# Gate units between the pair matrices and the inverses, an earlier decay chain, four gate buffers, and inverse roots by logarithm and exponent, in a two-layer hybrid trunk

## What is computed

```python
# one input projection of rms_norm(x), split among four branches and four sigmoid gates
# A: gated DeltaNet, chunks of 64
q, k = l2_normalize(q), l2_normalize(k)
g = -exp(a_log) * softplus(a + dt_bias)
gc = cumsum(g)                                  # within a chunk
m = where(strict, (k*beta) @ k.T * decay, 0)
t_inv = (eye + m)^-1                            # triangular
u, w = t_inv @ (v*beta), t_inv @ (k*beta*exp(gc))
# scan over chunks, then rms_norm(o) * silu(z)
# B: latent attention: rms_norm of the q and kv latents
# C: RWKV-7: l2_normalize(k * k_k), a delta rule with vector decay, group norm of o per head
# D: top-k sparse attention
out = w_o @ sum_b(sigmoid(gate_b) * (w_out_b @ branch_b))
x = x + out;  x = x + mlp(x)
```

## Time and profile before

| | us |
|---|---|
| median of 3 runs | 2272.09 (2271.6 to 2272.57) |
| the profiled execution | 2271.29 |
| its span in the profile | 2269.5 |
| PE busy | 2128.6 (94%) |
| DVE busy | 1238.7 (55%) |
| POOL busy | 732.9 (32%) |
| ACT busy | 720.8 (32%) |

### The profile page before, as it was taken

How to read it: one execution, slowest core, us unless ns; L and a number is a source line. 1 busy time by engine, 2 the same in 40 slices (tenths; PEclk the granted TensorE clock), 3 DMA queues, 4 the chain that set the end, 5 groups by cost and what they waited for, 6 DMA issues and landing times.

```text
span 2269.5 us, 34623 instructions
## 1 busy us (share of the span) xinstructions
PE 2128.6 (94%) x14488; PEld 1647.5 (73%) x14488; DVE 1238.7 (55%) x1930; ACT 720.8 (32%) x1100; POOL 732.9 (32%) x550
## 2 busy tenths in 40 slices
PE   5989899998999999999989898899899999999997
PEld 3778577765666788888868776877565678888886
DVE  6885765897563422222358766569956544222223
ACT  3421321332333332323243133123243334323322
POOL 1530221332213444444434012123223044444442
PEclk7999899998999999999989999999999999999998
DMA  4320111221121233332332001112212123323321
GB/s 159 106 70 15 56 30 41 82 68 58 45 96 61 84 111 97 97 93 94 94 105 90 27 26 55 36 60 71 64 54 97 34 81 99 95 93 95 100 93 65
DMA packets 52266, 170.03 MB, mean 75 GB/s; under 512 B 5648, under 2 KB 13968, under 8 KB 51600
## 3 DMA queue, kind: packets, MB, share of 16 engines
q1 hardware_dynamic: 50928, 162.75, 22.4%
q0 software_dynamic: 1184, 5.07, 0.6%
HBM read 160.45 MB, written 7.34 MB: 74 GB/s over the span
## 4 chain that ended last, share of the span: by engine, by line
PE 74%; DVE 21%; ACT 2%; issue 2%; DMA 1%; SPq 0%; DVEq 0%; ACTq 0%
PE bank_a L464 10%; PE bank_a L465 10%; PE bank_a L468 10%; PE bank_v L468 7%; PE bank_v L464 7%; PE bank_v L465 6%; PE bank_v L604 5%; PE bank_v L526 3%; DVE arena L1350 3%; DVE arena L1777 3%; DVE m L1775 2%; PE bank_v L720 2%; PE bank_v L702 1%; DVE arena L1768 1%; DVE mg L1356 1%
## 5 line engine op out<-in xcount | busy, mean ns | idle before, releaser
L425 POOL TENSOR_TENSOR w_lo<-ring,w_hi 128x512 fp32r<-128x512 f32 x536 | 726.4, 1377 | 1366.3 <-ACT w_hi L1064 1366.2
L464 PE MATMUL bank_a<-h_hi,w_hi 128*128 128x512 f32 x1376 | 561.3, 408 | 17.7 <-ACT w_hi L1064 12.5
L465 PE MATMUL bank_a<-h_lo,w_hi 128*128 128x512 f32 x1376 | 542.4, 394 | 0.0
L1064 ACT ACTIVATE w_hi<-ring 128x1024 fp32r<-128x1024 f32 x268 | 281.6, 1051 | 235.0 <-DVE arena L1892 220.5
L468 PE MATMUL bank_a<-h_hi,w_lo 128*128 128x512 f32 x1376 | 341.2, 390 | 0.0
L464 PEld LDWEIGHTS bank_a<-h_hi,w_hi 128*128 128x128 f32 x1376 | 261.5, 190 | 96.9 <-issue 18.0
L465 PEld LDWEIGHTS bank_a<-h_lo,w_hi 128*128 128x128 f32 x1376 | 262.3, 191 | 60.6 <-issue 8.1
L468 PEld LDWEIGHTS bank_a<-h_hi,w_lo 128*128 128x128 f32 x1376 | 259.1, 188 | 54.8 <-POOL w_lo L425 0.7
L1350 DVE TENSOR_TENSOR sg<-bank_v,sg 128x512 f32<-128x512 f32 x112 | 77.5, 692 | 339.6 <-PE bank_v L468 256.9
L464 PE MATMUL bank_v<-parts,w_hi 128*128 128x512 f32 x640 | 254.5, 398 | 1.4 <-DVE parts L1863 1.4
L465 PE MATMUL bank_v<-parts,w_hi 128*128 128x512 f32 x640 | 253.4, 396 | 0.0
(11 more groups left out here) (284 smaller groups left out, 2539.6 us busy)
## 6 DMA issues: line engine op xcount, KB each, us to landing
ring<-in_w SPq DMA_DIRECT2D x268, 512.0 KB, 3.5
out_ring<-in_w SPq DMA_DIRECT2D x64, 128.0 KB, 3.5
x_dram<-arena SPq DMA_DIRECT2D x2, 2048.0 KB, 7.6
arena<-x_dram SPq DMA_DIRECT2D x2, 2048.0 KB, 7.7
arena<-in_x SPq DMA_DIRECT2D x2, 1024.0 KB, 8.8
arena<-tabs POOLq DMA_DIRECT2D x4, 512.0 KB, 4.0
out_x<-arena SPq DMA_DIRECT2D x2, 1024.0 KB, 4.2
par<-in_par POOLq DMA_DIRECT2D x2, 937.0 KB, 7.2
```

Of the source, the lines that this page charges most:

```text
L425: ins = nc.gpsimd.tensor_tensor(w_lo[:, g % SPLIT, ks, :], raw, w_hi[:, g % SPLIT, ks, :].bitcast(F32), ALU.subtract)
L464: mm(b[:], w_hi[:, s, k, :], hi[:, k, :], start=k == 0, stop=False)
L465: mm(b[:], w_hi[:, s, k, :], lo[:, k, :], start=False, stop=False)
L1064: act_fn(w_hi[:, g % SPLIT, :, :], ring[:, g % RING, :, :], ACT.Copy).then_inc(S["split_hi"], 1)
```

## The change

- **Order of PE.** The first gate unit of the RWKV branch moves from behind the scan to between the second and the third pair call. The other gate units move up: after the scan come gates 1, 2 and 3 (three units where four were). Gate 7 of the RWKV branch moves behind the delta branch's pair calls, and the outputs of gates 6 and 7 follow it. `unit_list` is reordered to match, and ACT's and DVE's lists too.
- **Order of DVE.** `first_steps` is a function of its own. For the RWKV branch it runs after the second pair call's masks, ahead of the masks of `ark` and `arb`; for the delta branch after its masks, ahead of the merge of gates 6 and 7. The decay chain (L1675 to L1683) moves ahead of the first rule: its first part before the third convolution, its second behind the last; ACT's softplus moves behind the eviction of the fourth convolution input. The wide copies move ahead of the first merges.
- **Buffers.** `sg` has four tiles where it had two, and ACT waits for merge n - 4.
- **Head sums.** The five groups of sums (`r_l2`, `r_gv`, `g_l2`, `g_gv`, `m_nv`) go to a banks. ACT takes `Ln` with scale and epsilon straight from the bank and then one `Exp` with scale -0.5. DVE's scaling and reciprocal instructions and ACT's `Sqrt` are gone. In the delta branch's output norm this stands one unit earlier in ACT's list.
- The program is built with `dynamic_dma_scratch_size=8192`, and two constant columns are added. In layer 0 ACT waits once for the constants.

```diff
 def unit_list():
     u = [("rw", i) for i in range(8)] + [("misc", i) for i in range(2)]
-    u += [("gd", i) for i in range(8)]
-    u += [("merge", 2, i) for i in range(8)]
+    u += [("gd", i) for i in range(6)] + [("merge", 2, 0)]
+    u += [("gd", i) for i in range(6, 8)]
+    u += [("merge", 2, i) for i in range(1, 8)]
...
-        sg = sb("sg", [P, 2, T])
+        sg = sb("sg", [P, GATES, T])
...
                 pair_matrices(R["kd"], R["et"], "r")
+                numbers = [gate(l, 2, 0)]
                 pair_matrices(R["kd"], R["rt"], "r")
...
                 block_sums(l, "r_o", NC, R["o"], 2, "r_mean")
-                numbers = [gate(l, 2, 0)]
-                block_sums(l, "r_sq2", 1, R["sq"], 2, "r_gv")
                 numbers.append(gate(l, 2, 1))
-                block_sums(l, "g_sq", 1, G["sq"], 4, "g_l2")
-                more = gates(l, 2, 1)
+                block_sums(l, "r_sq2", 1, R["sq"], 2, "r_gv", "a")
+                more = [gate(l, 2, 2)]
+                block_sums(l, "g_sq", 1, G["sq"], 4, "g_l2", "a")
+                more.append(gate(l, 2, 3))
                 pe.wait_ge(S["r_out"], at(l, "r_out", 1))
...
                 merge(l, 2, 0, 2)
-                merge(l, 2, 0, 3)
+                numbers = [gate(l, 2, 6)]
                 pe.wait_ge(S["g_prep"], at(l, "g_prep", 1))
                 transposes((G["et"], G["vb"], G["bh"]), "g")
                 pair_matrices(G["co"][:, 2:4, :], G["kb"], "g")
                 pair_matrices(G["co"][:, 2:4, :], G["co"][:, 0:2, :], "g")
+                numbers.append(gate(l, 2, 7))
+                merge_outputs(0, numbers)
                 invert(l, "g", G, lambda n: None)
...
+            def inverse_roots(dst, scales, eps, sums, roots):
+                for i, scale in enumerate(scales):
+                    act.wait_ge(a_full, filled.next())
+                    b = filled.bank()
+                    act_fn(dst[:, i, :], b[:], ACT.Ln, scale=scale, bias=cst(eps)).then_inc(S[sums], 1)
+                act.wait_ge(S[sums], sums_done(sums, len(scales)))
+                act_fn(dst, dst, ACT.Exp, scale=-0.5).then_inc(S[roots], 1)
...
                     act_fn(G["ci"][:, i, :], b[:], ACT.Copy).then_inc(S["g_in"], 1)
                     split_next()
+                    if i == 3:
+                        act_fn(gsm[:, 5, :], ab[:, :, 4:8], ACT.Sigmoid)
+                        act.wait_ge(S["g_t1"], at(l, "g_t1", 1))
+                        act_fn(gsm[:, 1, :], gsm[:, 1, :], ACT.Exp).then_inc(act_step, 1)
+                        act_fn(sml[:, 8:12], pr("a_log"), ACT.Exp).then_inc(S["g_t2"], 1)
+                        act.wait_ge(act_step, l + 1)
+                        act_fn(gsm[:, 1, :], gsm[:, 1, :], ACT.Ln, bias=1.0).then_inc(S["g_sp"], 1)
...
-                merge_sig(l)
-                merge_sig(l)
+                merge_sig(l, 1)
+                inverse_roots(R["sq"], (1.0 / C, 1.0 / C), "gn_eps", "r_gv", "r_gs")
+                merge_sig(l, 1)
+                inverse_roots(G["rs"], (1.0,) * 4, "eps", "g_l2", "g_l2s")
+                merge_sig(l, 1)
...
                 for c in range(6):
+                    if c == 2:
+                        dve.wait_ge(S["ab_in"], at(l, "ab_in", 1))
+                        th = lambda i: gsm[:, i, :].rearrange("p (t h) -> p t h", h=H)
+                        tt(th(0), ab[:, :, 0:4], pr("dt").unsqueeze(1).to_broadcast([P, TT, H]), ADD)
+                        v.scalar_tensor_tensor(gsm[:, 1, :], gsm[:, 0, :], -1.0, gsm[:, 0, :], MUL, ALU.min).then_inc(S["g_t1"], 1)
+                        dve.wait_ge(S["g_t1"], reached("g_t1"))
+                        ts(ab[:, :, 8:16], ab[:, :, 8:16], float((8 * 64) ** -0.5), None, MUL)
                     conv(c)
+                dve.wait_ge(S["g_sp"], at(l, "g_sp", 1))
+                stt(gsm[:, 2, :], gsm[:, 0, :], 0.0, gsm[:, 1, :], ALU.max, ADD)
+                stt(th(4), th(2), -1.0, sml[:, 8:12].unsqueeze(1).to_broadcast([P, TT, H]), MUL, MUL)
                 masked("r", R["u"], lambda hp: wide("before_c"))
                 dve.wait_ge(S["r_tok"], at(l, "r_tok", 8))
                 masked("r", R["akk"], lambda hp: wide("before_c"))
+                first_steps("r", R)
                 masked("r", R["ark"], lambda hp: wide("upto_c"))
                 masked("r", R["arb"], lambda hp: wide("upto_c"))
...
-                    v.tensor_scalar(R["sq"][:, f, :], b[:], 1.0 / C, GN_EPS, MUL, ADD).then_inc(S["r_gv"], 1)
-                    dve.wait_ge(S["r_gv"], reached("r_gv"))
-                v.reciprocal(R["sq"], R["sq"]).then_inc(S["r_gr"], 1)
...
-                link(v.reciprocal(G["rs"][:, 2:4, :], G["rs"][:, 2:4, :]))
...
-    nc = bacc.Bacc("TRN2", target_bir_lowering=False, num_devices=1)
+    nc = bacc.Bacc("TRN2", target_bir_lowering=False, num_devices=1, dynamic_dma_scratch_size=8192)
```

More of the change, by code:

```diff
@@ L685, in scan, with block_sums @@
                     fill(c)
-            def block_sums(l, need, k, src, tiles, done):
+            def block_sums(l, need, k, src, tiles, done, pool="v"):
                 pe.wait_ge(S[need], at(l, need, k))
                 for i in range(tiles):
-                    b, reader, emptied = banks.next("v", done)
+                    b, reader, emptied = banks.next(pool, done)
                     pe.wait_ge(reader, emptied)
-                    mm(b[:], cst("blocks"), src[:, i, :], start=True, stop=True).then_inc(v_full, 1)
+                    mm(b[:], cst("blocks"), src[:, i, :], start=True, stop=True).then_inc(a_full if pool == "a" else v_full, 1)
             def attention(l, x, q_of, k_of, v, fill):
@@ L889, in _ @@
                 pe.wait_ge(S["m_sq"], at(l, "m_sq", 1))
-                b, reader, emptied = banks.next("v", "m_nv")
+                b, reader, emptied = banks.next("a", "m_nv")
                 pe.wait_ge(reader, emptied)
@@ L893, in _ @@
                     ins = mm(b[:], cst("ones"), Mv["sq"][:, k, :], start=k == 0, stop=k == 1)
-                ins.then_inc(v_full, 1)
-                b, reader, emptied = banks.next("v", "m_nv")
+                ins.then_inc(a_full, 1)
+                b, reader, emptied = banks.next("a", "m_nv")
                 pe.wait_ge(reader, emptied)
-                mm(b[:], cst("ones"), Mv["sq"][:, 2, :], start=True, stop=True).then_inc(v_full, 1)
+                mm(b[:], cst("ones"), Mv["sq"][:, 2, :], start=True, stop=True).then_inc(a_full, 1)
                 merge(l, 3, 0, 2)
@@ L1052, in late_sig @@
                     n = sigs[0]
[L1053 removed]
+                    act_fn(sg[:, n % GATES, :], sg[:, n % GATES, :], ACT.Sigmoid).then_inc(S["mg_sig"], 1)
                     sigs[0] += 1
@@ L1143, in _ @@
                 take_low_rank("g", None)
+                inverse_roots(R["tmp"], (1.0, 1.0), "eps", "r_l2", "r_l2s")
                 take_rw(5)
-                act.wait_ge(S["r_l2r"], at(l, "r_l2r", 1))
-                act_fn(R["tmp"], R["tmp"], ACT.Sqrt).then_inc(S["r_l2s"], 1)
                 take_rw(6)
@@ L1417, in invert @@
                     dve.wait_ge(S[x + "_x1"], reached(x + "_x1"))
+            def invert(l, x, V, fill):
+                halves = [slice(half * M // 2, (half + 1) * M // 2) for half in range(2)]
                 for n, s in enumerate(LEVELS):
@@ L1576, in _ @@
                 mix(4)
-                for f in range(2):
-                    dve.wait_ge(v_full, filled.next())
-                    b = filled.bank()
-                    v.tensor_scalar(R["tmp"][:, f, :], b[:], EPS, None, ADD).then_inc(S["r_l2"], 1)
-                    dve.wait_ge(S["r_l2"], reached("r_l2"))
-                v.reciprocal(R["tmp"], R["tmp"]).then_inc(S["r_l2r"], 1)
-                dve.wait_ge(S["r_l2r"], reached("r_l2r"))
                 mix(5)
@@ L1725, in _ @@
                 dve.wait_ge(S["g_sq2"], reached("g_sq2"))
-                for f in range(2):
-                    dve.wait_ge(v_full, filled.next())
-                    b = filled.bank()
-                    v.tensor_scalar(G["sq2"][:, f, :], b[:], 1.0 / C, EPS, MUL, ADD).then_inc(S["g_gv"], 1)
-                    dve.wait_ge(S["g_gv"], reached("g_gv"))
-                v.reciprocal(G["sq2"], G["sq2"]).then_inc(S["g_gr"], 1)
-                dve.wait_ge(S["g_gr"], reached("g_gr"))
                 dve.wait_ge(S["g_gs"], at(l, "g_gs", 1))
```

108 lines of the change are left out of this document (38 added, 70 removed).

## The result

The changed kernel takes 2219.24 us (median of 4 runs, 2217.08 to 2219.4) beside 2272.33 us for the kernel before in the same session: ratio 0.9762, 95% interval 0.9749 to 0.9774. The forecast was 2216, the range 2203 to 2236. 53 us are gone where 56 were forecast.

The account below looks back on a forecast made before the run. PE, busy 94% of the span, was taken as the bound. Per layer 1.9 (gap one) + 5.44 (unit) + 20.1 (gap two's stalls) + 0.4 = 27.8 us, twice 55.7, gave 2216 us, range 2203 to 2236.

Parts of the forecast that it names:

- Gap two: PE's stretch from RWKV scan to delta inverse: stalls gone, gain 20.1 us a layer, plus 5.44 for the moved unit.
- all three stalls: In gap two: w_hi 5.12 us plus 2.2 cold; decay tiles 6.19 plus 2.8; before the inverse 3.6 plus 1.8.
- The one new wait: At the fourth g_l2 sum, PE waits for a bank that ACT empties late: 1.6 us a layer.
- Gap one: PE ahead of the RWKV inverse: 14.0 us shrinks to 12.1 with a gate unit inside, gaining 1.9 a layer.
- The rest: Outside both gaps: only the L859 wait behind the delta output norm goes, 0.4 us a layer; other parts 0.
- L702 stays: At the attention's start: DVE bounds up to there, so PE's wait of 9.3 us in 4 stays unchanged.
- the 0 for the buffers: Four gate buffers free ACT from merges but gain PE nothing beyond the w_hi waits: 0 us.
- become late: Rival, chance 0.24: ACT's in-order queue runs late; 5 us a layer gives 2226, 10 us gives 2236.
- its two figures: By the skill's rules: drains at table switches make the sum 2227; one load for exp and ln lowers it 2.6 us.
- Only displaces: Rival, chance 0.07: DVE's masks come 5 us later, PE still waits, gap one gives nothing: 2231.
- the slower one: Rival, chance 0.03: smaller scratch brings the first parameter load in portions, delaying DVE's first norm; 16 portions give 2299.
- DVE's lead carries on: Rival, chance 0.15: DVE's 4.7 us lead from the delta output norm reaches the top-k: 2207.

Follow-up runs that it names:

- g1: Changed kernel with three gate buffers in place of four: 2218.11 us, ratio 0.9753 to the kernel before.
- u2: Changed kernel with the r_gv and g_l2 head sums again through DVE's addition and reciprocal and ScalarE's root: 2245.66 us, ratio 0.9877.
- u5: Changed kernel with the sums of the delta output norm and latent norms again through DVE's reciprocal and ScalarE's root: 2217.67 us, ratio 0.9761.
- s2: Changed kernel with the first index scores, their rectifications and the fourth rotation product one unit earlier: 2218.4 us, ratio 0.9756.
- u1: Changed kernel with the gate unit between the RWKV pair matrices put back behind the scan: 2226.53 us, ratio 0.979.
- c1: The kernel before with only the smaller scratch for POOL's DMA descriptors: 2273.31 us, ratio 1.0003.
- second profile: Profile of the changed kernel run again unedited in another session: 2217.73 us, ratio 0.9761 to the kernel before.
- s4: Changed kernel with later q/k sums, all index scores ahead of outputs, selections ahead of merges, latent units ahead of second outputs: 2233.1 us, ratio 0.9826.
- s1: Changed kernel with three q/k sums moved behind the fourth gate unit and the last between the two outputs: 2214.8 us, ratio 0.9741.

## Why the prediction was right

- **Gap two, its stalls and the unit (5.44 + 20.1 = 25.5 us a layer forecast).** Measured 24.9 and 25.7. Here the time was, and all three stalls went with their cold clock. The one new wait came at the place and with the size worked out (1.66 us; forecast 1.6), so the working of ScalarE's order held: the root was ready at 240.3 us, forecast 239.2, and the sums ahead of it start 1.08 us later too (240.83, in the old times 239.75). The output chain took 5.9 us (240.41 to 246.27), not 8.5; no wait hung on it.
- **Its parts.** Undone one at a time, unit, sums, decay chain and last gate cost 6.4, 26.1, 12.0 and 5.9 us, together 50 of the 54 us (0.0238 of 2272), each known to some 4 us: no large overlap shows. The buffers' share does not show in the total (g1). The prediction was right that the w_hi wait is ScalarE's root held by DVE's reciprocal. What failed is u2's expectation that it comes back at the same place: it moved to the outputs.
- **Gap one (1.9 us a layer).** From the second pair call to DVE's first level step it is 12.08 us (152.89 to 164.97; forecast 12.1), partly by luck: the decay chain cost DVE some 1 us less than taken, and an instruction beside POOL's split 1 us more. The inverse behind it adds small waits. From the transposes to the end of the inverse, the two layers gained 0.5 and 2.9 us in the first profile, 1.8 and 2.3 in the second (51.7 and 52.6 before).
- **The rest (0.4 a layer).** From delta to the last output matmul of the attention (L723) layer 0 gained 1.1 us and layer 1 lost 0.8: PE waits longer ahead of the scores (L705) and 1.6 us a layer less at L713 behind them. The wait L859 went as forecast (0.8 us in 2), but the index scores' waits grew by 0.6 in both layers together. By u5 none of it is the output norm's. The reason given (DVE bounds from the selection to the attention) was half right: s2 shows that PE takes a lead of DVE away once more, at the first output. "L702 stays" and the 0 for the buffers were wrong steps that cancel: g1 shows that the fourth buffer lengthens the wait ahead of the attention and shortens the attention by about as much. That they cancel is luck.
- **The rivals.** ScalarE did not become late: its new waits are 1.66 us at the sums and 0.77 at the delta transposes. The Trainium skill's drain of 1.38 us behind a table load (ScalarE: Activation LUTs, What ACT_TABLE_LOAD costs) is not in this trace: load at 240.33, sigmoid at 241.62. One load for exp and ln, as the same page has it (Table sets: the hidden batching unit), did not come either, so neither of its two figures (2227, 2.6 us less) came. "Only displaces" fell with u1, the slower one with c1, "DVE's lead carries on" with u5.
- **The 3 us short of the forecast.** In the profiled execution some 2.8 us are lost by the end of the RWKV inverse of layer 0, which another execution of the same kernel lacks; but that one's span is only 1.3 us shorter, so at most a part of the shortfall is this. The 1 to 1.8 us between delta and attention in both layers are the fourth buffer's: they are there with the old output sums (u5: 179.5 and 180.7 us), are all but gone with three (g1: 177.0 and 178.3), and the attention gives about as much back. The shortfall of the medians stays in part unexplained; it is about as large as the measurement's doubt.
- **The range and the signs.** The lower end of the range is 2203, but the sum beside it gives 2201; its 10.2 us of cold clock and the upper end's "low bounds" are not worked out, so the range rests on less than the forecast. Of the signs, L705 is not unchanged (11.7 us against 9.3), and a wait of 2.56 us for w_hi stayed, at 56.4 us, outside both gaps. The end of the delta inverse came 23.9 us earlier in layer 0, and 26.7 in the second profile; the sign said some 27.

## What to carry to other kernels

When a slow operation of one engine (here a reciprocal of 6.55 us) feeds several consumers, PE's waits name whichever stands first in PE's order; price the operation, not the wait. A lead gained on an engine off the critical path is worth what its next inputs allow: follow it to the next place where it needs the bound engine before counting it, and test it, since moving that place can cost more than it brings (s4). A wait made by an order of work over few banks could here be had back by placing other work between (s1, 2 us a layer). A run without an effect on the total can hide two effects: compare its stretches as well (g1).

## What was not expected of the hardware

An elementwise DVE instruction with both inputs in SBUF (128x512) took 1.67 us in place of 0.69 when it started beside POOL's split of w_lo, in the second profile 1.69; the four masks behind it, with one input in PSUM, took 2.87 us together (0.72 each), though the first of them still ran beside POOL. The Trainium skill (GPSIMD Engine Reference, 1. Specifications) says that GpSimd shares its way to SBUF with VectorE and contends with instructions of two SBUF inputs; the trace agrees. The same happens ahead of the attention (g1 above): a scan of 512 columns took 2.17 us in place of 1.23.

A DVE instruction of 16 columns took 0.18 us at its new place, with POOL idle, and 1.18 us in the kernel before, while POOL worked on w_lo (265.94 to 270.88 us). So a small instruction's duration in one profile was a bad price for others of its kind.

The same unit behind a short wait had the clock at 1.00 in one execution and at 0.77 in another, a mean between the levels 1.2 and 2.4 GHz (waits 1.41 and 2.56 us), worth 1.5 us: two profiles of a kernel can differ by more than a small edit brings.
